# A hybrid decoder block on one core: the recurrence's gate products as three fp32r products of halves instead of one f32 product

## The chip, the cores and the metric

One of the eight cores of a Trainium2 chip runs one launch of the kernel. The metric is the device time of that launch in microseconds (us); lower is better. TensorE is called PE in the rows, its weight load PEld, VectorE DVE, ScalarE ACT, GpSimd POOL and SyncE SP.

## The reference, cut to what matters

One layer over 256 tokens of width 2048: a mixer (retention heads beside a gated linear recurrence, the RG-LRU), cross-attention into 256 memory tokens, a gated feed-forward part with a convolution, and norms between them. All is f32. The change is in the two gates of the RG-LRU:

```
def rg_lru(u, w_a, b_a, w_x, b_x, lam):
    ub = uf.reshape(B, S, LRU_BLOCKS, LRU_BLOCK_DIM)          # 8 blocks of 128
    r = sigmoid(einsum('bsnc,ncd->bsnd', ub, w_a) + b_a)
    i = sigmoid(einsum('bsnc,ncd->bsnd', ub, w_x) + b_x)
    log_a = LRU_C * r * log_sigmoid(lam)
    a = exp(log_a)
    b = sqrt(-expm1(2.0 * log_a)) * (i * uf)
    ... scan over the tokens: h = a * h + b
```

`u` is a causal convolution (4 taps) of a projection of the normed input. So each of 8 blocks needs two products of a 128x128 weight with a 128x256 input.

## The kernel before, in words

All weights of the large products come as one stream of panels, 128 partitions by 1024 f32, in the order of their use. SP loads a panel into one of four slots of `raw`; ACT copies it, rounded to fp32r, into `whi` (`split` at L560); DVE subtracts and writes the rest into `wlo` (`split` at L916). A product with f32 accuracy is then three fp32r products, high by high, high by low, low by high. A chunk is two panels; `narrow` (L273) is one chunk against all 256 tokens: 32 products, 16 of 512 columns (high half of the weight by both halves of the input) and 16 of 256 columns. `wide` (L290) does the same with weight and input exchanged.

Every engine has its own program, written out by hand, and semaphores between them. On ACT and DVE, `step(m, pr, do0, do1, do2)` waits until TensorE has used a pair of panels, calls `do0`, splits the first new panel, calls `do1`, splits the second, calls `do2`. An engine does its program strictly in the written order. The side work of a stage (copies, norms, taps) hangs in these three places.

The stage of the recurrence's projections is a loop over the 8 blocks, `n` from 0 to 7; one pass has two steps, for the chunk of `u` and the chunk of `y`:

- ACT, first step: `u0` asks for the block's gate weights (`gw`, a part of `dmask`, 128x256: both gates side by side) and copies half of the product's sum out of PSUM (`copy_hl`, L575); `u1` makes the first term of the convolution (L686). Second step: `copy_hl` again, then `y1` after `gates_done`: three tanh (L692 to L694); `y2` the gelu (L698).
- DVE, first step: `u0` adds the halves and scales (L934, L1096); `u1` adds the other three taps into `scr[:, 3]` (L1102) and signals `uc_ready`. Second step: `y0` (L934, L1111) and `y1` (L1117).
- TensorE: `gates_of(n)` (L382) stands inside the `narrow` of the next block, after its first 12 products, and for the last block after the first panel of the value projection that follows. It waits for `uc_ready` and for the weights, and makes two f32 products of 256 columns into `bankA`:

```
mm(bankA[:, :T], gw[:, :P], scr[:, 3, :], True, True)
mm(bankA[:, T:], gw[:, P:], scr[:, 3, :], True, True).then_inc(gates_done, 1)
```

The cross-attention, later, has products of the same form as the new ones: `scores` (L461) and `attend` (L481), fp32r halves with 256 columns.

Of the kernel before, what the change touches and what calls it, by code (L numbers as in the profile page):

```python
# [29 lines left out]
ALU = mybir.AluOpType  # L30
ACT = mybir.ActivationFunctionType
# [3 lines left out]
P = 128  # L35
D = 2048
T = 256
# [18 lines left out]
C_YU = C_KM + KT  # L56
# [60 lines left out]
def build(nc, stream, cols, xin, memin, xt_in, memt_in, first_in, pos, gates, decay, ident_in, gfin_in, out):  # L117
    with ExitStack() as ctx:
        def sb(name, shape, dt=F32):
            return ctx.enter_context(nc.sbuf_tensor(name, shape, dt))  # L120

        def sem(name):
            return ctx.enter_context(nc.semaphore(name))
# [24 lines left out]
        with ExitStack() as early:  # L148
            gel, dmask, scrg, scr, vbuf = (early.enter_context(nc.sbuf_tensor(n, shape, F32)) for n, shape in (
                ("gel", [P, LB, T]), ("dmask", [P, RH, T]), ("scrg", [P, 4, T]), ("scr", [P, 8, T]), ("vbuf", [P, TT, R])))  # L150
        k_head, q_hi, q_lo = sb("k_head", [P, 2, 4, T], F32R), sb("q_hi", [P, 4, T], F32R), sb("q_lo", [P, 4, T], F32R)
        sb("scr_low", [P, 2, T])
        p_head = sb("p_head", [P, 2, 2, T], F32R)
        sb("scr_high", [P, 2, T])
        v_heads = sb("v_heads", [P, 2, TT, XD], F32R)

        mem_rows = [b[:].rearrange("p a b -> p (a b)") for b in (vbuf, gel)]
        lru_t = xres[:, 0, :].rearrange("p (n t) -> p n t", n=LB)
# [3 lines left out]
        gw = dmask[:, 0, :]  # L162
# [7 lines left out]
        bankA, bankB = ps[:, 6, :], ps[:, 7, :]  # L170
# [16 lines left out]
        gw_in, un_ready, uc0_done, uc_ready, yn_ready, gates_done, i_ready = (  # L187
            sem(n) for n in ("gw_in", "un_ready", "uc0_done", "uc_ready", "yn_ready", "gates_done", "i_ready"))
# [9 lines left out]
        qT_ready, sc_done, nb_ready, p_ready, pn_ready, pt_done, pT_ready, v_ready, pv_done, ot_hi, ot_lo = (  # L198
            sem(n) for n in ("qT_ready", "sc_done", "nb_ready", "p_ready", "pn_ready", "pt_done", "pT_ready", "v_ready",
                             "pv_done", "ot_hi", "ot_lo"))  # L200
        q_sum, q_hi_done, k_hi_done, k_ready, p_hi_done, v_hi_done = (
            sem(n) for n in ("q_sum", "q_hi_done", "k_hi_done", "k_ready", "p_hi_done", "v_hi_done"))
        up_ready, cv_done, cva_ready, sil_done, hh_ready, hh_hi, hh_lo = (
# [4 lines left out]
        def f32(ap):  # L208
            return ap.bitcast(F32)
# [59 lines left out]
        def _(pe):  # L269
            def mm(o, l, r, start, stop):  # L270
                return nc.tensor.matmul(o, l, r, start=start, stop=stop, skip_group_check=True)  # L271
# [109 lines left out]

            def gates_of(n1):  # L382

                pe.wait_ge(uc_ready, n1)
                pe.wait_ge(gw_in, 16 * n1)
                mm(bankA[:, :T], gw[:, :P], scr[:, 3, :], True, True)
                mm(bankA[:, T:], gw[:, P:], scr[:, 3, :], True, True).then_inc(gates_done, 1)

            pe.wait_ge(xt_lo, KT - 2)
            narrow(C_YU // 2, 0, xT, {KT - 2: lambda: pe.wait_ge(xt_lo, KT)})  # L390
# [1 line left out]
            with pe.Fori(1, LB) as n:  # L392
                narrow(C_YU // 2 + n, 0, xT, {6: lambda: gates_of(n)})
                narrow(C_YU // 2 + n, 1, xT)

            for n, (g, kp) in enumerate(WIDE_ORDER):
                wide(C_V // 2 + n // 2, n % 2, xT, range(4 * kp, 4 * kp + 4), 2 * g, kp == 0, kp == 3,
                     None if n else lambda: gates_of(LB))
# [138 lines left out]
            for tt in range(TT):  # L537
                for n in range(2):
                    for k in range(GF):
                        if tt == 0 and k % 2 == 0:  # L540
                            pe.wait_ge(lo_done, 2 * NC - 4 + 2 * n + k // 2 + 1)
                        w = slice(k % 2 * CG, (k % 2 + 1) * CG)
# [4 lines left out]
                        last = mm(ps[:, 2 * n + tt, :], x_lo, hi, False, k == GF - 1)  # L547
# [4 lines left out]
        def _(act):  # L552
            ch = Chain(act, chain_a)
            A = nc.scalar.activation

            def split(m, pr, s):

                act.wait_ge(raw_landed[2 * pr + s], 16 * m + 32)
                act.wait_ge(panels_used, 4 * m + (2 * pr + s + 1))
                A(whi[:, 2 * pr + s, :], raw[:, 2 * pr + s, :], ACT.Copy).then_inc(hi_done, 1)  # L560

            def step(m, pr, do0=None, do1=None, do2=None):

                act.wait_ge(panels_used, 4 * m + (2 * pr + 2))
                if do0:
                    do0()
                split(m, pr, 0)
                if do1:
                    do1()
                split(m, pr, 1)  # L570
                if do2:
                    do2()

            def copy_hl(pr):
                A(hl[:, pr, :], ps[:, 4 + pr, T:], ACT.Copy).then_inc(hl_copied, 1)  # L575
# [101 lines left out]
            with act.Fori(0, LB) as n:  # L677
                ch.reg = n

                def u0():  # L680
                    act.dma_start(gw, gates[n]).then_inc(gw_in, 16)
                    copy_hl(0)

                def u1():
                    act.wait_ge(un_ready, n + 1)
                    A(scr[:, 3, :], scr[:, 2, :], ACT.Identity, scale=par[:, ds(4 * n + (O_CW + 3), 1)],  # L686
                      bias=par[:, ds(n + O_CB, 1)]).then_inc(uc0_done, 1)

                def y1():

                    act.wait_ge(gates_done, n + 1)
                    ch.link(A(scr[:, 4, :], bankA[:, :T], ACT.Tanh, scale=0.5, bias=halves[:, ds(n, 1)]))  # L692
                    A(scr[:, 5, :], bankA[:, T:], ACT.Tanh, scale=0.5, bias=halves[:, ds(n + LB, 1)]).then_inc(i_ready, 1)
                    ch.mark(A(lru_t[:, n, :], scr[:, 4, :], ACT.Tanh, scale=cs[:, ds(n, 1)], bias=cs[:, ds(n, 1)]))  # L694

                def y2():
                    act.wait_ge(yn_ready, n + 1)
                    A(gel[:, n, :], scr[:, 6, :], ACT.Gelu_apprx_tanh)  # L698

                step(C_YU // 2 + n, 0, u0, u1)  # L700
                step(C_YU // 2 + n, 1, lambda: copy_hl(1), y1, y2)
            ch.leave(LB)

# [206 lines left out]
        def _(dve):  # L910
            V = nc.vector
            ch = Chain(dve, chain_v)

            def split(m, pr, s):
                dve.wait_ge(hi_done, 4 * m + (2 * pr + s + 5))
                V.tensor_tensor(wlo[:, 2 * pr + s, :], raw[:, 2 * pr + s, :], f32(whi[:, 2 * pr + s, :]),  # L916
                                ALU.subtract).then_inc(lo_done, 1)

            def step(m, pr, do0=None, do1=None, do2=None):

                dve.wait_ge(panels_used, 4 * m + (2 * pr + 2))
                if do0:
                    do0()
                split(m, pr, 0)
                if do1:
                    do1()
                split(m, pr, 1)
                if do2:
                    do2()

            def narrow_sum(w, pr, dst):

                dve.wait_ge(hl_copied, w + 1)
                return V.tensor_tensor(dst, ps[:, 4 + pr, :T], hl[:, pr, :], ALU.add)  # L934
# [156 lines left out]
            with dve.Fori(0, LB) as n:  # L1091
                ch.reg = n

                def u0():
                    ch.link(narrow_sum(W_YU + 2 * n, 0, tmp[:, 0, :]))
                    V.tensor_tensor(scr[:, 2, :], tmp[:, 0, :], row[:], ALU.mult).then_inc(un_ready, 1)  # L1096

                def u1():
                    dve.wait_ge(uc0_done, n + 1)
                    for tap in (2, 1, 0):  # L1100
                        sh = 3 - tap
                        ins = V.scalar_tensor_tensor(out=scr[:, 3, sh:], in0=scr[:, 2, :T - sh],  # L1102
                                                     scalar=par[:, ds(4 * n + (O_CW + tap), 1)], in1=scr[:, 3, sh:],
                                                     op0=ALU.mult, op1=ALU.add)
                        if tap:
                            ch.link(ins)
                    ins.then_inc(uc_ready, 1)

                def y0():
                    ch.link(narrow_sum(W_YU + 2 * n + 1, 1, tmp[:, 1, :]))  # L1110
                    V.tensor_tensor(scr[:, 6, :], tmp[:, 1, :], row[:], ALU.mult).then_inc(yn_ready, 1)  # L1111

                def y1():
                    dve.wait_ge(i_ready, n + 1)
                    dve.wait_ge(uc_ready, n + 1)

                    V.scalar_tensor_tensor(out=lru_gx[:, n, :], in0=scr[:, 5, :], scalar=1.0, in1=scr[:, 3, :],  # L1117
                                           op0=ALU.add, op1=ALU.mult)

                step(C_YU // 2 + n, 0, u0, u1)  # L1120
                step(C_YU // 2 + n, 1, y0, y1)
            ch.leave(LB)

# [404 lines left out]
```

## Time and profile before

| what | value |
|---|---|
| median of 3 runs | 1505.83 us (1505.77 to 1506.15) |
| profiled execution | 1505.75 us |
| its span, first to last instruction | 1504.0 us |
| busy: PE, DVE, ACT | 1494.7, 1076.4, 818.5 us |
| granted TensorE clock, mean | 0.999 |
| the recurrence stage | about 188 to 284 us |

The profiled execution is taken by the hardware profiler; its own time is 1.75 us above its span. A clock of 1.00 is the full 2.4 GHz. In a timeline row stand start, length, engine, line, operation, output and inputs with shapes; a row with xN is N instructions in a row, its length from the first start to the last end. What stands in square brackets is the idle time before it and what ended it. Names like `scr` or `dmask` are the program's tensors, `ps` is PSUM. f32 and fp32r inputs of TensorE both read "f32".

### The profile page before, as it was taken

Reading aid. Unit: us, or ns where it says so; the run is one execution under the profiler, and the core shown is the slowest. Engines: PE = TensorE matmul, PEld = TensorE weight load, DVE = VectorE, ACT = ScalarE, POOL = GpSimd, SP = SyncE. Lnnn points to the kernel's source line nnn. Section 1 sums busy time; section 2 is a strip of 40 time slices with the busy share of each in tenths; the row PEclk is TensorE's granted clock in tenths of the full one; section 3 lists DMA queues with packets and bytes.
Section 4 is the critical chain, followed back from the end, with each engine's and each line's share of the span. In section 5 each row is a group of like instructions: output and inputs, shape, how many; then the busy total and the mean of one; then the engine's idle time right before and its main releaser. Section 6 shows DMA issues by size and latency. Waiting matters only on the chain.

```text
span 1504.0 us, 24205 instructions
## 1 busy us (share of the span) xinstructions
PE 1494.7 (99%) x7926; PEld 1282.6 (85%) x7926; DVE 1076.4 (72%) x1577; ACT 818.5 (54%) x1185; POOL 2.9 (0%) x9
## 2 busy tenths in 40 slices
PE   9999999999999999999999999999999999999997
PEld 8888888888888888888888888888888888888886
DVE  6756666788887556655578777777777777777876
ACT  6644478644555546544575455454645455454654
POOL 0000000000000000000000000000000000000000
PEclk9999999999999999999999999999999999999999
DMA  9766655655556554446556555555555555555553
GB/s 349 251 204 210 209 183 189 202 186 168 173 177 237 182 184 166 144 156 200 181 169 198 186 193 189 195 186 187 191 188 196 188 187 190 195 184 193 184 194 140
DMA packets 80458, 288.89 MB, mean 192 GB/s; under 512 B 8944, under 2 KB 10480, under 8 KB 79520
## 3 DMA queue, kind: packets, MB, share of 16 engines
q1 hardware_dynamic: 76176, 275.68, 55.3%
q10 hardware_dynamic: 3744, 9.30, 1.8%
q0 software_dynamic: 496, 3.34, 0.6%
q8 instruction: 27, 0.44, 0.1%
q14 instruction: 15, 0.12, 0.0%
HBM read 286.19 MB, written 2.10 MB: 192 GB/s over the span
## 4 chain that ended last, share of the span: by engine, by line
PE 97%; DVE 1%; ACT 1%; issue 0%; DMA 0%; ACTq 0%; DVEq 0%
PE ps L271 97%; PE ps L328 0%; DVE wlo L916 0%; ACT whi L560 0%; DVE vm L1399 0%; DMA hl<-in_first_in 0%; DVE xres L1409 0%; PE ps L423 0%; ACT scr L800 0%; ACT scr L893 0%; DVE sm_ L1268 0%; DVE xres L1372 0%; ACT vm L906 0%; PE ps L477 0%; DVE tmp L934 0%
## 5 line engine op out<-in xcount | busy, mean ns | idle before, releaser
L271 PE MATMUL ps<-xT,whi 128*128 128x512 f32 x2304 | 727.5, 397 | 0.2
L916 DVE TENSOR_TENSOR wlo<-raw,whi 128x1024 fp32r<-128x1024 f32 x516 | 623.0, 1221 | 127.5 <-ACT whi L560 117.9
L560 ACT ACTIVATE whi<-raw 128x1024 fp32r<-128x1024 f32 x516 | 531.8, 1050 | 224.3 <-PE ps L271 219.4
L271 PEld LDWEIGHTS ps<-xT,wlo 128*128 128x128 f32 x2304 | 432.8, 188 | 102.0
L271 PE MATMUL ps<-whi,mixT 128*128 128x512 f32 x1472 | 457.6, 390 | 0.2 <-ACT whi L601 0.2
L271 PE MATMUL ps<-xT,wlo 128*128 128x256 f32 x2304 | 453.0, 278 | 0.0
L271 PEld LDWEIGHTS ps<-xT,whi 128*128 128x128 f32 x2304 | 352.6, 189 | 2.3 <-DVE wlo L916 0.8
L271 PEld LDWEIGHTS ps<-whi,mixT 128*128 128x128 f32 x1472 | 276.3, 188 | 57.8 <-issue 0.6
L271 PE MATMUL ps<-wlo,mixT 128*128 128x512 f32 x736 | 285.2, 389 | 0.0
L575 ACT ACTIVATE hl<-ps 128x256 f32<-128x256 f32 x160 | 61.5, 384 | 236.6 <-PE ps L271 236.5
L934 DVE TENSOR_TENSOR tmp<-ps,hl 128x256 f32<-128x256 f32 x160 | 67.7, 423 | 146.3 <-ACT hl L575 146.0
L271 PEld LDWEIGHTS ps<-wlo,mixT 128*128 128x128 f32 x736 | 138.1, 188 | 27.8 <-DVE wlo L975 0.2
L1372 DVE TENSOR_TENSOR xres<-ps,xres 128x512 f32<-128x512 f32 x84 | 54.1, 686 | 60.5 <-PE ps L271 59.3
L1335 DVE SCALAR_TENSOR_TENSOR tmp<-tmp,par 128x255 f32<-128x255 f32 (+1 forms) x176 | 84.6, 481 | 11.1 <-DVE tmp L1335 1.5
L271 PE MATMUL ps<-mixT,whi 128*128 128x512 f32 x256 | 80.4, 395 | 0.0
L854 ACT ACTIVATE tmp<-tmp,par 128x256 f32<-128x256 f32 x88 | 53.0, 603 | 18.7 <-DVE tmp L1328 17.6
L271 PEld LDWEIGHTS ps<-mixT,wlo 128*128 128x128 f32 x256 | 48.1, 188 | 11.4
L863 ACT ACTIVATE mixT<-scr 128x256 fp32r<-128x256 f32 x44 | 18.4, 418 | 68.6 <-DVE scr L1345 39.1
L271 PE MATMUL ps<-mixT,wlo 128*128 128x256 f32 x256 | 50.3, 278 | 0.0
L271 PE MATMUL ps<-whi,xT 128*128 128x512 f32 x128 | 39.9, 391 | 0.0
L1328 DVE TENSOR_TENSOR tmp<-tmp,row 128x256 f32<-128x256 f32 x88 | 37.4, 425 | 3.0
L271 PEld LDWEIGHTS ps<-mixT,whi 128*128 128x128 f32 x256 | 39.0, 189 | 0.1
(177 smaller groups left out, 645.7 us busy)
## 6 DMA issues: line engine op xcount, KB each, us to landing
raw<-in_stream SPq DMA_DIRECT2D x518, 512.0 KB, 3.3
xres<-in_xin ACTq DMA_DIRECT2D x2, 1024.0 KB, 7.9
scr<-in_xt_in ACTq DMA_DIRECT2D x8, 256.0 KB, 3.6
xres<-in_xin POOLq DMA_DIRECT2D x1, 2048.0 KB, 9.9
out_x<-vm SPq DMA_DIRECT2D x4, 512.0 KB, 3.1
raw<-in_stream SPq DMA_DIRECT2D x4, 256.0 KB, 4.2
kT<-in_memt_in ACTq DMA_DIRECT2D x2, 512.0 KB, 5.3
vbuf<-in_memin ACTq DMA_DIRECT2D x1, 1024.0 KB, 9.7
```

What stands on the lines that cost most here:

```text
L271: return nc.tensor.matmul(o, l, r, start=start, stop=stop, skip_group_check=True)
L560: A(whi[:, 2 * pr + s, :], raw[:, 2 * pr + s, :], ACT.Copy).then_inc(hi_done, 1)
L575: A(hl[:, pr, :], ps[:, 4 + pr, T:], ACT.Copy).then_inc(hl_copied, 1)
L854: A(tmp[:, 2 + ab, :], tmp[:, ab, :], ACT.Identity, scale=par[:, ds(4 * u + (O_FC + 2), 1)], bias=par[:, ds(4 * u + (O_FC + 3), 1)]).then_ ...
L863: A(mixT[:, k0 + k, 0, :], hold[:, k % 2, :], ACT.Copy).then_inc(hh_hi, 1)
L916: V.tensor_tensor(wlo[:, 2 * pr + s, :], raw[:, 2 * pr + s, :], f32(whi[:, 2 * pr + s, :]), ALU.subtract).then_inc(lo_done, 1)
L934: return V.tensor_tensor(dst, ps[:, 4 + pr, :T], hl[:, pr, :], ALU.add)
L1328: V.tensor_tensor(tmp[:, ab, :], tmp[:, 5, :], row[:], ALU.mult).then_inc(up_ready, 1)
L1335: ins = V.scalar_tensor_tensor(out=tmp[:, 2 + ab, sh:], in0=tmp[:, ab, :T - sh], scalar=par[:, ds(4 * u + (O_FC + tap), 1)], in1=tmp[:, 2 ...
L1372: V.tensor_tensor(x, ps[:, 2 * (n % 2) + tt, :], x, ALU.add).then_inc(fin_added, 1)
```

## The change

The gate weights and the convolved input are each split in a high and a low half, into a buffer that lies idle in this stage (`q_lo`, whose place is that of `scrg`). ACT writes the high halves (two more copies a block), DVE the low halves (two more subtractions), both in the third place of the first step, and TensorE makes three fp32r products for each gate. It waits for one new semaphore, `gate_ready`, which DVE raises after the second subtraction. The weights' landing is now waited for by ACT.

```diff
+        gw_parts, u_parts = q_lo[:, 0:2, :], q_lo[:, 2:4, :]
...
+        gw_hi_done, u_hi_done, gate_ready = sem("gw_hi_done"), sem("u_hi_done"), sem("gate_ready")
...
             def gates_of(n1):
 
-                pe.wait_ge(uc_ready, n1)
-                pe.wait_ge(gw_in, 16 * n1)
-                mm(bankA[:, :T], gw[:, :P], scr[:, 3, :], True, True)
-                mm(bankA[:, T:], gw[:, P:], scr[:, 3, :], True, True).then_inc(gates_done, 1)
+                pe.wait_ge(gate_ready, n1)
+                for j in range(2):
+                    o, w = bankA[:, j * T:(j + 1) * T], slice(j * P, (j + 1) * P)
+                    mm(o, gw_parts[:, 0, w], u_parts[:, 0, :], True, False)
+                    mm(o, gw_parts[:, 0, w], u_parts[:, 1, :], False, False)
+                    last = mm(o, gw_parts[:, 1, w], u_parts[:, 0, :], False, True)
+                last.then_inc(gates_done, 1)
...
+                def u2():
+                    act.wait_ge(gw_in, 16 * n + 16)
+                    A(gw_parts[:, 0, :], gw, ACT.Copy).then_inc(gw_hi_done, 1)
+                    act.wait_ge(uc_ready, n + 1)
+                    A(u_parts[:, 0, :], scr[:, 3, :], ACT.Copy).then_inc(u_hi_done, 1)
...
-                step(C_YU // 2 + n, 0, u0, u1)
+                step(C_YU // 2 + n, 0, u0, u1, u2)
...
+                def u2():
+                    dve.wait_ge(gw_hi_done, n + 1)
+                    V.tensor_tensor(gw_parts[:, 1, :], gw, f32(gw_parts[:, 0, :]), ALU.subtract)
+                    dve.wait_ge(u_hi_done, n + 1)
+                    V.tensor_tensor(u_parts[:, 1, :], scr[:, 3, :], f32(u_parts[:, 0, :]), ALU.subtract).then_inc(gate_ready, 1)
...
-                step(C_YU // 2 + n, 0, u0, u1)
+                step(C_YU // 2 + n, 0, u0, u1, u2)
```

The order on DVE between the third tap (`scr<-scr,par 128x253`) and the scaling in `y0`, in the loop over the blocks, before and then changed (line numbers of the changed kernel are 2 to 17 higher):

```order
L1102 SCALAR_TENSOR_TENSOR scr<-scr,par 128x253
L915 REGISTER_ALU
L916 TENSOR_TENSOR wlo<-raw,whi 128x1024 [waits hi_done]
L921 REGISTER_ALU
L933 REGISTER_ALU [waits panels_used]
L934 TENSOR_TENSOR tmp<-ps,hl 128x256 [waits hl_copied]
L96 REGISTER_ALU
L1111 TENSOR_TENSOR scr<-tmp,row 128x256 [waits chain_v]
```

```order
L1113 SCALAR_TENSOR_TENSOR scr<-scr,par 128x253
L926 REGISTER_ALU
L927 TENSOR_TENSOR wlo<-raw,whi 128x1024 [waits hi_done]
L1122 TENSOR_TENSOR q_lo<-dmask,q_lo 128x256 [waits gw_hi_done]
L1124 TENSOR_TENSOR q_lo<-scr,q_lo 128x256 [waits u_hi_done]
L932 REGISTER_ALU
L944 REGISTER_ALU [waits panels_used]
L945 TENSOR_TENSOR tmp<-ps,hl 128x256 [waits hl_copied]
L96 REGISTER_ALU
L1128 TENSOR_TENSOR scr<-tmp,row 128x256 [waits chain_v]
```

Between the tap and the second subtraction, whose end TensorE now waits for, stand a panel's split and the first subtraction.

The order on ACT from the first term of the convolution to the tanh, changed kernel (`q_lo` is the buffer of the halves, `dmask` holds the gate weights):

```order
L691 ACTIVATE scr<-scr,par 128x256
L565 ACTIVATE whi<-raw 128x1024 [waits panels_used,raw_landed1]
L695 ISA
L696 ACTIVATE q_lo<-dmask 128x256 [waits gw_in]
L698 ACTIVATE q_lo<-scr 128x256 [waits uc_ready]
L569 REGISTER_ALU
L580 ACTIVATE hl<-ps 128x256 [waits panels_used]
L564 REGISTER_ALU [waits raw_landed2]
L565 ACTIVATE whi<-raw 128x1024 [waits panels_used]
L703 REGISTER_ALU [waits gates_done]
L703 ACTIVATE scr<-ps,halves 128x256
```

The two copies stand ahead of the hl copy and of the third split, which before followed the second split at once.

## Rows read from the trace of the kernel before

**Rows 1.** The first page: the span, and TensorE's busy time
```profile
span 1504.0 us, 24205 instructions
...
PE 1494.7 (99%) x7926; PEld 1282.6 (85%) x7926; DVE 1076.4 (72%) x1577; ACT 818.5 (54%) x1185; POOL 2.9 (0%) x9
```

**Rows 2.** Chain that ended last, 188 to 284 us: start, length, what
```profile
187.84 96.29 PE ps L271 x538
```

**Rows 3.** Busy time in two stretches: PE, PEld, DVE, ACT, POOL, then PE clock, DMA
```profile
0.00:10.00 10.00, 8.84 (x38) 7.80 (x39) 4.40 (x8) 6.10 (x11) 1.61 (x7) 1.00 0.79 282
188.00:284.00 96.00, 96.00 (x539) 83.57 (x538) 64.01 (x96) 74.49 (x102) 0.00 (x0) 1.00 0.56 184
```

**Rows 4.** Instructions on tile dmask: durations in ns, first and last start
```profile
L271 PE MATMUL ps<-scr,dmask x32: 377/378/379, 196.0 to 281.5; 128*128 128x256 f32 x32
...
DMA to landing us min/median/max: 2.2/3.5/5.5
```

**Rows 5.** Timeline of PE around one block's gates: start, length, engine, line, operation
```profile
255.44 0.63 PE L271 MATMUL ps<-xT,whi 128*128 128x512 f32 x2
255.91 0.40 PE L271 MATMUL ps<-xT,wlo 128*128 128x256 f32 x2
256.14 1.02 PE L271 MATMUL ps<-scr,dmask 128*128 128x256 f32 x4
...
257.47 0.40 PE L271 MATMUL ps<-xT,wlo 128*128 128x256 f32 x2
```

**Rows 6.** Timeline of PE around the attention's products of halves
```profile
599.94 3.02 PE L271 MATMUL ps<-p_head,v_heads 128*128 128x256 f32 x24
602.80 0.63 PE L271 MATMUL ps<-xT,whi 128*128 128x512 f32 x2
```

**Rows 7.** Timeline of PE, gate products of blocks 1, 5 and 8
```profile
196.04 1.02 PE L271 MATMUL ps<-scr,dmask 128*128 128x256 f32 x4
...
244.12 1.02 PE L271 MATMUL ps<-scr,dmask 128*128 128x256 f32 x4
...
280.82 1.02 PE L271 MATMUL ps<-scr,dmask 128*128 128x256 f32 x4
```

**Rows 8.** Timeline of ACT in one pass
```profile
245.28 0.47 ACT L692 ACTIVATE scr<-ps,halves 128x256 f32<-128x256 f32 x1 [1.72 <-PE ps L271]
...
248.81 0.34 ACTq L681 DMA_DIRECT2D dmask<-in_gates  x1
...
250.84 0.39 ACT L575 ACTIVATE hl<-ps 128x256 f32<-128x256 f32 x1
...
252.89 1.05 ACT L560 ACTIVATE whi<-raw 128x1024 fp32r<-128x1024 f32 x1
```

**Rows 9.** Timeline of DVE in the same pass
```profile
251.25 0.42 DVE L934 TENSOR_TENSOR tmp<-ps,hl 128x256 f32<-128x256 f32 x1 [2.19 <-ACT hl L575]
...
253.97 1.11 DVE L1102 SCALAR_TENSOR_TENSOR scr<-scr,par 128x254 f32<-128x254 f32 x2 [0.15 <-DVE scr L1102]
255.00 1.22 DVE L916 TENSOR_TENSOR wlo<-raw,whi 128x1024 fp32r<-128x1024 f32 x1
256.14 0.42 DVE L934 TENSOR_TENSOR tmp<-ps,hl 128x256 f32<-128x256 f32 x1
256.59 0.42 DVE L1111 TENSOR_TENSOR scr<-tmp,row 128x256 f32<-128x256 f32 x1
256.93 1.22 DVE L916 TENSOR_TENSOR wlo<-raw,whi 128x1024 fp32r<-128x1024 f32 x1
```

**Rows 10.** Timeline of DVE in the first pass: the split behind the taps
```profile
194.54 1.22 DVE L916 TENSOR_TENSOR wlo<-raw,whi 128x1024 fp32r<-128x1024 f32 x1
```

**Rows 11.** Timeline around a wait of TensorE for a DVE split
```profile
10.50 2.48 DVE L975 TENSOR_TENSOR wlo<-raw,whi 128x1024 fp32r<-128x1024 f32 x2 [1.00 <-ACT whi L605]
...
11.78 0.30 PEld L271 LDWEIGHTS ps<-wlo,mixT 128*128 128x128 f32 x2 [0.17 <-DVE wlo L975]
11.86 0.42 PE L271 MATMUL ps<-wlo,mixT 128*128 128x512 f32 x1
```

## The prediction

> **What bounds the kernel now.** I read the first page's busy shares and the chain of waits, then the stretch that the change touches. TensorE is busy for 1494.7 of 1504.0 us [rows 1], and in the stretch of the eight recurrence blocks (188 to 284 us) the chain that ended last is TensorE alone, with no wait in it [rows 2]. The table of that stretch says the same: PE 96.00 of 96.00 us, at the full granted clock of 1.00, with DVE at 64.01 and ACT at 74.49 [rows 3]. So one microsecond of TensorE saved here is one saved in the end, and any wait put into TensorE's stream here is lost in full, since nothing behind it stands idle to give it back. What has to be found is therefore two numbers: how much shorter the gate products get, and how late their inputs come.
>
> **Part 1, the products on TensorE.** Per block, two f32 products become six fp32r ones, all 256 columns wide. Before, the records show four entries of 377 to 379 ns for the two products (32 for the 16 of all eight blocks [rows 4]). In the sequence of TensorE a group opens with two products on the high half, the two on the low half start 0.47 us later (255.44 to 255.91), and the next group would open at 256.14. There the gate products stand, and that group's low half starts at 257.47 instead of 256.61: the two f32 products cost 257.47 - 256.14 - 0.47 = 0.86 us [rows 5]. The new shape has a row too: 24 products of 256 columns with fp32r halves in the attention fill 599.94 to 602.80, 2.86 / 24 = 0.119 us each [rows 6]. Six cost 0.715 us. Saving: 0.86 - 0.715 = 0.145 us a block, 8 x 0.145 = 1.2 us at most.
>
> The Trainium skill (FP8 and Floating Point Precision, TensorE Precision Notes) says that true FP32 takes 4 passes through the array, high and low halves against each other. The trace agrees as far as it goes: at 0.107 us for 256 columns at 2.4 GHz the pair's 0.86 us is eight passes. By that rule alone, three passes instead of four would save a quarter, 0.215 us a block or 1.7 us in all, and the sum below would be +4.6 us; I keep the 0.119 us of the row, which has the weight loads in it.
>
> **Part 2, where the inputs come from.** Before, the gate products waited for the third tap of the convolution alone (`uc_ready`). Now they wait for `gate_ready`, at the end of this: ACT copies the weights (128x256), waits for `uc_ready`, copies the convolved input; DVE takes first its next split of a weight panel (1.22 us), and only then the two subtractions. I follow the pass from 244.12 to 256.14.
>
> - Third tap: the last two taps run from 253.97 for 1.11 us, to 255.08. Room before TensorE asks, at 256.14: 1.06 us [rows 5, 9].
> - ACT's copies: its second split ends at 252.89 + 1.05 = 253.94 [rows 8]; the weights are asked for at 248.81 and land after 2.2 to 5.5 us [rows 4], by 254.3 at worst. A copy of 128x256 costs 0.39 us (the hl row [rows 8]): weights done by 254.7, the input's copy from 255.1 to 255.5. ACT's next work, another hl copy and a split, moves behind them: 255.5 + 0.39 + 1.05 = 256.9, before the gate products have begun. Off the path.
> - DVE: split from 255.00, next operation 1.14 us later at 256.14 [rows 9]. First subtraction 256.14, second 0.34 us later (the distance between an operation of 0.42 us and an independent next one, 256.59 to 256.93 [rows 9]), done at 256.48 + 0.42 = 256.90. ACT's copies are ready by then.
> - TensorE takes it up: at 11.78 a weight load starts some 0.04 us after the first of two DVE splits that released it (10.50 + 2.48 / 2 = 11.74), the product 0.08 us behind it [rows 11]. I take 0.15 us. First gate product at 257.05, against 256.14: late by 0.91 us.
>
> **Part 3, whether the wait repeats.** If only the inputs were late once, TensorE would slip by 0.9 us and be on time afterwards. But the next block's inputs hang on this block's gates. From the gates' end ACT has no pause: tanh at 245.28, three of them, a split, two loads of an activation table around the gelu, and the hl copy at 250.84 only when all this is done [rows 8]. DVE stood idle for 2.19 us for that very copy [rows 9]. Then follow the sum, the scaling, a split, the taps, the split and now the subtractions. So it is a closed loop: gates of block n, ACT's queue, DVE's queue, gates of block n+1. Before, its length was 255.08 - 244.12 = 10.96 us to `uc_ready`, and TensorE's own pass of 12.02 us (244.12 to 256.14 [rows 5, 7]) was the longer. Now it is:
>
>   257.05 - 244.12 = 12.93, less what the gates give back. Before, the tanh started 245.28 - 244.12 = 1.16 us after the first product. Six products at 0.119 put the last start at 0.60, its end 0.28 us later (3.02 - 23 x 0.119 [rows 6]) at 0.88, and the same 0.14 us to ACT makes 1.02. So 12.93 - 0.14 = **12.79 us**, against 11.87 that TensorE itself would need (12.02 - 0.145). The loop is the longer one, by 0.92 us a pass.
>
> **The sum.**
> - Block 1: third tap and split are at 194.54 [rows 10]; subtractions done at 194.54 + 1.14 + 0.34 + 0.42 = 196.44, first product at 196.59 instead of 196.04 [rows 7]: +0.55.
> - Blocks 2 to 7: six passes of 12.79 instead of 12.02: 6 x 0.77 = +4.62.
> - Block 8: its gates stand in the first panel of the value projection, 2.7 us into it instead of 2.1. 280.82 [rows 7] less 268.16 (196.04 + 6 x 12.02) is 12.66; the loop's 12.79 still wins: +0.13.
> - The last products: -0.145.
> Together 0.55 + 4.62 + 0.13 - 0.15 = **+5.15 us**. Counted the other way: waits 0.55 + 6 x 0.92 + 0.27 = 6.3 us, savings 1.2 us. After block 8 nothing else is changed, and TensorE carries the delay to the end.
>
> The profiled execution took 1505.75 us for its span of 1504.0; 1505.75 + 5.15 = 1510.9. The median of the runs is 1505.83, so the two stand together within 0.1 us. A measurement of this kernel can tell about 0.2%, 3.0 us, from no change; the forecast is above that.
>
> **Bounds of the unknown terms.** TensorE's start: 0.04 to 0.3 us. Distance of the two subtractions: 0.34, or 0.45 as between chained operations (256.14 to 256.59 [rows 9]). Tanh after the gates: the 0.14 us gain may be eaten by weight loads that cannot run ahead while TensorE waits. Low: 0.11 less on each of seven steps and 0.1 off the first, +4.3 us. High: 0.15 + 0.11 + 0.14 = 0.40 more on seven steps, 0.26 on the first, +8.2 us. I take the middle of the rows nearest to the new operations.
>
> **Rivals.**
> - *The room of 1.06 us covers it.* If the subtractions come before DVE's split, or nothing is late, only the saving is left: 1505.75 - 1.2 = 1504.6, no change that can be measured. For it: ACT and DVE are busy for only 78% and 67% of the stretch [rows 3]. Against: the order on DVE is fixed, and 1.14 + 0.34 + 0.42 after 255.00 is past 256.14 whatever the averages. It decides if `gate_ready` comes within 1.06 us of `uc_ready`; I count 1.82. Chance 0.08.
> - *The wait is paid once.* If the hl copy of the next block does not hang on the tanh, TensorE slips by 0.9 us once and saves 1.2: 1505.5. Against: ACT's rows from 245.28 to 250.84 have no gap. Chance 0.06.
> - *TensorE loses its clock.* Each pass would hold a stop of 0.9 us. The granted clock is 1.00 in the stretch and also in the first 10 us, where 1.16 us were idle [rows 3]. If a quarter of the stretch's 90 us ran at 1.2 instead of 2.4 GHz, it would take 22 us more: 1533. The Trainium skill (TensorE: Matmul & The Clock Gate, A second HAM failure mode: psum-queue depth-cycling) says that frequent short idles between groups of products can make the clock swing between its two levels. The row with 1.16 us idle in 10 speaks against it here. Chance 0.02.
> - *The loop is longer than I count*, at the high bound or beyond it: 1514. Chance 0.07, mostly inside the range.
>
> **How the numbers follow.** The forecast (a loop of about 12.8 us, seven times) has 0.77, and the predicted time is its 1510.9. The range takes its bounds, 1510.0 and 1514.0, with 0.6 us more below for a shorter wait on block 8 and on the first: 1509.4 to 1514.0. Left out are the first three rivals, 0.16, and little beyond the high bound. Slower by over 3.0 us: forecast, long loop and clock, 0.86. Within 0.2%: the first two rivals, 0.14, of which 0.01 goes to faster, for which I have no mechanism.
>
> **What would show it.** The view to read is TensorE from 188 to 290 us: eight waits before the gate products, released by DVE's second subtraction, about 0.55, 0.9 (six times) and 0.3 us, 6 us together; starts 12.8 us apart instead of 12.0; DVE's second subtraction ending 1.8 us behind the third tap; ACT without a gap from the tanh to the hl copy; the six products about 0.7 us; clock 1.00. No waits, or one only, would make me wrong, and so would starts 12.0 us apart.

## The result, and the profile after

The changed kernel takes 1511.11 us (median of 7 runs, 1510.81 to 1511.43), the kernel before beside it 1506.04 us (1505.75 to 1506.48): 5.1 us more, a ratio of 1.0034 with a 95% interval of 1.0025 to 1.0043. The forecast was 1510.9 us, in a range of 1509.4 to 1514.0. The profiled execution has a span of 1509.1 us where before had 1504.0 [rows 1].

The first page and the stretch of the recurrence, in the rows that answer to [rows 1] and [rows 3]; the stretch reaches to 290 us, since the stage is now longer:

```profile
span 1509.1 us, 24269 instructions
...
PE 1495.2 (99%) x7942; PEld 1282.4 (85%) x7942; DVE 1082.3 (72%) x1593; ACT 823.5 (55%) x1201; POOL 2.9 (0%) x9
```

```profile
188.00:290.00 102.00, 97.84 (x558) 84.35 (x557) 69.84 (x114) 80.19 (x119) 0.00 (x0) 1.00 0.51 175
```

TensorE's busy time has hardly moved (1494.7 us before), the span is 5.1 us longer, and 4.2 of the 102 us of the stretch are idle on TensorE, at a granted clock of 1.00 as before. The view of waits in that stretch names what it waits for (engine and line, released by, us in total, times, longest):

```profile
PEld ps L273 <- DVE q_lo L1124: 6.0, 8, 0.9
PE ps L273 <- DVE q_lo L1124: 4.2, 7, 0.7
```

L1124 is DVE's second subtraction. The weight-load row counts each wait from the end of the last load (6.0 us in eight waits), the product row from the modelled end of the last product, which lies later (4.2 us). The timeline of one pass of the changed kernel, TensorE's rows first (these answer to [rows 5, 7]):

```profile
234.93 0.98 PE L273 MATMUL ps<-q_lo 128*128 128x256 f32 x6 [0.64 <-DVE q_lo L1124]
247.71 0.98 PE L273 MATMUL ps<-q_lo 128*128 128x256 f32 x6 [0.64 <-DVE q_lo L1124]
247.71 0.77 PEld L273 LDWEIGHTS ps<-q_lo 128*128 128x128 f32 x6 [0.84 <-DVE q_lo L1124]
248.53 0.64 PE L273 MATMUL ps<-xT,whi 128*128 128x512 f32 x2
```

The first and the last group of gate products in the same trace:

```profile
196.61 0.97 PE L273 MATMUL ps<-q_lo 128*128 128x256 f32 x6 [0.29 <-DVE q_lo L1124]
...
286.05 0.98 PE L273 MATMUL ps<-q_lo 128*128 128x256 f32 x6
```

Then DVE and ACT around them (these answer to [rows 8, 9]):

```profile
244.74 1.11 DVE L1113 SCALAR_TENSOR_TENSOR scr<-scr,par 128x254 f32<-128x254 f32 x2 [0.15 <-DVE scr L1113]
245.77 1.22 DVE L927 TENSOR_TENSOR wlo<-raw,whi 128x1024 fp32r<-128x1024 f32 x1
245.88 0.42 ACT L698 ACTIVATE q_lo<-scr 128x256 fp32r<-128x256 f32 x1 [0.87 <-DVE scr L1113]
246.90 0.42 DVE L1122 TENSOR_TENSOR q_lo<-dmask,q_lo 128x256 fp32r<-128x256 f32 x1
247.24 0.42 DVE L1124 TENSOR_TENSOR q_lo<-scr,q_lo 128x256 fp32r<-128x256 f32 x1
248.82 0.47 ACT L703 ACTIVATE scr<-ps,halves 128x256 f32<-128x256 f32 x1 [1.30 <-PE ps L273]
```

```profile
250.30 1.05 ACT L565 ACTIVATE whi<-raw 128x1024 fp32r<-128x1024 f32 x1
251.37 1.28 ACT L709 ACT_TABLE_LOAD   x1
252.36 0.34 ACTq L686 DMA_DIRECT2D dmask<-in_gates  x1
252.66 0.42 ACT L709 ACTIVATE gel<-scr 128x256 f32 x1
253.08 1.28 ACT L580 ACT_TABLE_LOAD   x1
254.38 0.38 ACT L580 ACTIVATE hl<-ps 128x256 f32<-128x256 f32 x1
```

The passes are 247.71 - 234.93 = 12.78 us apart instead of 12.02. The third tap is done at 245.85, ACT's copy of the input at 246.30, and then that copy lies unused for 0.94 us, because DVE is in the split of a panel and then in the first subtraction. TensorE starts 0.05 us behind the end of the second one. On ACT there is no gap from the first tanh to the hl copy, 248.82 to 254.38; the rows of the other two tanh are left out above.

### The profile page after: what moved, and what is told of

The parts are those of the page before. It is cut to its first block, busy times and chain, and to the rows that moved or that the text cites. A ratio compares the mean times of both kernels' runs of the same rounds, so it can differ in the third digit from the quotient of the medians.

```text
span 1509.1 us, 24269 instructions
## 1 busy us (share of the span) xinstructions
PE 1495.2 (99%) x7942; PEld 1282.4 (85%) x7942; DVE 1082.3 (72%) x1593; ACT 823.5 (55%) x1201; POOL 2.9 (0%) x9
## 4 chain that ended last, share of the span: by engine, by line
PE 92%; ACT 3%; DVE 2%; issue 1%; ACTq 0%; DMA 0%; DVEq 0%
PE ps L273 91%; ACT whi L565 1%; DVE wlo L927 1%; ACT L580 1%; DVE scr L1113 0%; PE ps L330 0%; ACT L709 0%; ACT scr L691 0%; DVE vm L1416 0%; DMA hl<-in_first_in 0%; DVE q_lo L1122 0%; ACT scr L703 0%; ACT hl L580 0%; ACTq L686 0%; DVE xres L1426 0%
```

## The experiments

Ten kernels ran. One theory had to be told from three others. The closed loop: gates, ACT's queue, DVE's queue, next gates are one ring, and whatever is longer, ring or TensorE's own pass, sets the time of a pass. Against it: added work costs wherever it stands; the new products themselves are dear; the lateness is fixed in each block and has nothing to do with ACT's queue. The expectations count the kernels in the order in which they were built: the fourth is the one with the gelu out of the loop, the sixth and the seventh have the useless copy, in the changed kernel and in the kernel before.

### Subtractions ahead of the split

```diff
                     ins.then_inc(uc_ready, 1)
+                    dve.wait_ge(gw_hi_done, n + 1)
+                    V.tensor_tensor(gw_parts[:, 1, :], gw, f32(gw_parts[:, 0, :]), ALU.subtract)
+                    dve.wait_ge(u_hi_done, n + 1)
+                    V.tensor_tensor(u_parts[:, 1, :], scr[:, 3, :], f32(u_parts[:, 0, :]), ALU.subtract).then_inc(gate_ready, 1)
...
-                step(C_YU // 2 + n, 0, u0, u1, u2)
+                step(C_YU // 2 + n, 0, u0, u1)
```

> The changed kernel with DVE's two subtractions directly behind the third tap, ahead of the second split of a weight panel. Closed-loop theory: in the changed kernel the second subtraction starts 1.39 us behind the end of the third tap (245.85 to 247.24); here it starts as soon as ACT's copy of the input is done, about 0.50 us behind it, so the loop falls from 12.77 to about 11.9 us, a tie with TensorE's own pass of 11.87. The waits nearly vanish, the time is 1504.6 to 1505.6 us, 5.5 to 6.5 below the changed kernel and 0.2 to 1.2 below the kernel before. Rival, that the delay is the mere work added on ACT and DVE, wherever it stands: same work, so no change from the changed kernel, 1511. Rival, that the six products themselves are dearer than the row of the attention says: still above 1508.

Measured: 1504.93 us (11 runs, 1504.56 to 1505.54), before 1505.96; ratio 0.9993, interval 0.9984 to 1.0002. No wait of TensorE in the stretch. DVE and TensorE in this run:

```profile
253.68 1.11 DVE L1113 SCALAR_TENSOR_TENSOR scr<-scr,par 128x254 f32<-128x254 f32 x2 [0.15 <-DVE scr L1113]
254.70 0.42 DVE L1120 TENSOR_TENSOR q_lo<-dmask,q_lo 128x256 fp32r<-128x256 f32 x1
255.27 0.43 DVE L1122 TENSOR_TENSOR q_lo<-scr,q_lo 128x256 fp32r<-128x256 f32 x1 [0.15 <-ACT q_lo L698]
255.61 1.22 DVE L927 TENSOR_TENSOR wlo<-raw,whi 128x1024 fp32r<-128x1024 f32 x1
```

```profile
243.96 0.89 PE L273 MATMUL ps<-q_lo 128*128 128x256 f32 x6
255.84 0.89 PE L273 MATMUL ps<-q_lo 128*128 128x256 f32 x6
```

The first subtraction lies in the time in which DVE has to wait for ACT's copy anyway; the second ends at 255.70, the products start at 255.84 with no bracket behind them, and the pass is 11.88 us. All the work of the change is still done. So with ACT's queue as it is, it is not the work but its place in DVE's queue that costs 6.2 us (1511.11 - 1504.93).

### The wait kept, the f32 products back

```diff
                 pe.wait_ge(gate_ready, n1)
-                for j in range(2):
-                    o, w = bankA[:, j * T:(j + 1) * T], slice(j * P, (j + 1) * P)
-                    mm(o, gw_parts[:, 0, w], u_parts[:, 0, :], True, False)
-                    mm(o, gw_parts[:, 0, w], u_parts[:, 1, :], False, False)
-                    last = mm(o, gw_parts[:, 1, w], u_parts[:, 0, :], False, True)
-                last.then_inc(gates_done, 1)
+                mm(bankA[:, :T], gw[:, :P], scr[:, 3, :], True, True)
+                mm(bankA[:, T:], gw[:, P:], scr[:, 3, :], True, True).then_inc(gates_done, 1)
```

> The changed kernel, all copies, subtractions and the wait for gate_ready kept, but TensorE makes the two f32 products of before. Closed-loop theory: the products' part of the loop grows back by 0.1 to 0.14 us, so 12.9 us a pass, and the saving of 1.2 us is gone: 1512.0 to 1512.4 us, 0.9 to 1.3 above the changed kernel. If the new products were what costs the time, this would be near 1506.

Measured: 1512.17 us (5 runs, 1512.00 to 1512.63), ratio 1.0043, interval 1.0029 to 1.0056. Its passes:

```profile
235.25 1.13 PE L273 MATMUL ps<-scr,dmask 128*128 128x256 f32 x4 [0.66 <-DVE q_lo L1120]
248.18 1.13 PE L273 MATMUL ps<-scr,dmask 128*128 128x256 f32 x4 [0.66 <-DVE q_lo L1120]
```

12.93 us apart, 0.15 more than with the fp32r products. The wait alone is worth 6.2 us, and the products give 1.1 us of it back.

### The products alone

```diff
-                pe.wait_ge(gate_ready, n1)
+                pe.wait_ge(uc_ready, n1)
+                pe.wait_ge(gw_in, 16 * n1)
...
+            for j in range(8):
+                A(q_lo[:, j // 2, (j % 2) * P:(j % 2 + 1) * P], ones[:], ACT.Copy)
             act.wait_ge(halves_set, 1)
...
-                def u2():
```

(Shown against the changed kernel. `u2` is gone from both engines, so the halves are not made: the kernel leaves out the gates' values and its output is not that of the layer.)

> The kernel before with six fp32r products in place of the two f32 ones, waiting as before for uc_ready and the weights. The halves are left out: the products read a buffer filled once with ones, so the gates' values are left out of the computation. Closed-loop theory: no wait appears, the products cost 0.70 to 0.72 us instead of 0.86, TensorE's pass is 11.87 us, and the time is 1504.6 us, 1.2 below the kernel before (ratio 0.9992). If the products in this place cost what they do in the changed kernel's trace (0.82 us from the first product to the next group's), the gain is 0.3 us: 1505.5.

Measured: 1504.82 us (11 runs, 1504.59 to 1505.29), ratio 0.9992, interval 0.9983 to 1.0001. The products of a pass and the group behind them:

```profile
219.92 0.79 PEld L273 LDWEIGHTS ps<-q_lo 128*128 128x128 f32 x6
220.04 0.88 PE L273 MATMUL ps<-q_lo 128*128 128x256 f32 x6
220.75 0.63 PE L273 MATMUL ps<-xT,whi 128*128 128x512 f32 x2
221.04 0.48 ACT L700 ACTIVATE scr<-ps,halves 128x256 f32<-128x256 f32 x1 [1.57 <-PE ps L273]
```

0.71 us, and passes of 11.87 us (231.91 - 220.04 in the same view). This is all that the change can give: 1.1 us, and the first experiment gets nearly the same, 1.0 us, with the work of the splits in it. Both intervals still hold a ratio of 1, so the medians alone do not show a gain. The passes do: from the first to the eighth group of gate products it is 84.78 us in the kernel before (196.04 to 280.82), 83.75 us here and 83.81 us in the first experiment.

### The gelu out of the loop

```diff
-                def y2():
-                    act.wait_ge(yn_ready, n + 1)
-                    A(gel[:, n, :], scr[:, 6, :], ACT.Gelu_apprx_tanh)
...
+            def gelus(n0):
+                act.wait_ge(yn_ready, LB)
+                A(gel[:, n0:n0 + 4, :], gel[:, n0:n0 + 4, :], ACT.Gelu_apprx_tanh)
+
+            gelus(0)
...
-                    step(C_V // 2 + n // 2, 0, None, lambda: lru_root(n // 2))
+                    step(C_V // 2 + n // 2, 0, None, lambda: lru_root(n // 2), (lambda: gelus(4)) if n == 6 else None)
...
-                    V.tensor_tensor(scr[:, 6, :], tmp[:, 1, :], row[:], ALU.mult).then_inc(yn_ready, 1)
+                    V.tensor_tensor(gel[:, n, :], tmp[:, 1, :], row[:], ALU.mult).then_inc(yn_ready, 1)
```

> The changed kernel with the gelu taken out of the loop over the blocks (two instructions of four blocks each behind it), so that the gelu and the two table loads around it, 3.0 us, leave ACT's queue between the gates and the next hl copy. Nothing on the gates' inputs is changed. Closed-loop theory: the loop is 12.77 - 3.0 = 9.8 us, shorter than TensorE's pass, so all waits for gate_ready go and only the saving is left: 1504.6 us, at most 1.5 more if the gelus behind the loop delay a split. Rival, a fixed lateness of gate_ready that does not depend on ACT's queue (paid in each block since the inputs are 1.8 us behind the tap): the waits stay, 1511.

Measured: 1509.03 us (11 runs, 1508.66 to 1509.18), ratio 1.0020, interval 1.0011 to 1.0029. A miss by 4.4 us: only 2.1 us of the loss came back. The waits of TensorE are 0.28 us each in the timeline, and the passes 12.40. ACT shows why:

```profile
224.12 1.05 ACT L565 ACTIVATE whi<-raw 128x1024 fp32r<-128x1024 f32 x1
226.16 0.34 ACTq L686 DMA_DIRECT2D dmask<-in_gates  x1
226.54 1.28 ACT L580 ACT_TABLE_LOAD   x1 [1.36 <-PE ps L273]
227.83 0.39 ACT L580 ACTIVATE hl<-ps 128x256 f32<-128x256 f32 x1
```

One table load has stayed. It belongs to the hl copy at the head of the loop's body, and it cannot start before the copy's own wait, for TensorE's use of the panels. So the ring has changed its course: no longer by the tanh, but gates, the 20 products behind them, this load, hl copy, DVE. The hl copy stands 227.83 - 221.54 = 6.29 us behind the gates, against 254.38 - 247.71 = 6.67 us in the changed kernel: 0.38 us less, as the passes are. The sum in my expectation had taken both loads out.

### The same without the last table load

```diff
             act.wait_ge(halves_set, 1)
+            A(scr[:, 6, :8], ones[:, :8], ACT.Tanh)
             ch.enter(0, 2)
```

On top of the edit of the fourth run. The load then stands once, ahead of the loop (its row is in the last section).

> The changed kernel with the gelu out of the loop, as in the fourth run, plus one small tanh on ACT (128x8) ahead of the loop, so that no table load is left inside it. The fourth run kept one load a pass: it stood in front of the hl copy and began only when TensorE had used the panels (226.54 in that trace, hl copy at 227.83), and the passes were 12.40 us. Closed-loop theory, with this load as the rest of the loop: without it the hl copy comes 1.28 us sooner, gate_ready 12.40 - 1.28 = 11.12 us behind the gates before, under TensorE's 11.87; no wait is left and the time is 1504.8 to 1505.4 us. If the load is not what held the loop there, the passes stay at 12.4 us and the time at 1509.

Measured: 1504.85 us (11 runs, 1504.71 to 1505.02), before 1505.86; ratio 0.9993, interval 0.9983 to 1.0002. ACT now, and TensorE's passes of 11.87 us without a wait:

```profile
224.65 0.39 ACT L580 ACTIVATE hl<-ps 128x256 f32<-128x256 f32 x1 [1.40 <-PE ps L273]
224.94 1.05 ACT L565 ACTIVATE whi<-raw 128x1024 fp32r<-128x1024 f32 x1
```

```profile
219.72 0.88 PE L273 MATMUL ps<-q_lo 128*128 128x256 f32 x6
231.59 0.88 PE L273 MATMUL ps<-q_lo 128*128 128x256 f32 x6
```

```profile
227.79 1.11 DVE L1116 SCALAR_TENSOR_TENSOR scr<-scr,par 128x254 f32<-128x254 f32 x2 [0.15 <-DVE scr L1116]
228.82 1.22 DVE L930 TENSOR_TENSOR wlo<-raw,whi 128x1024 fp32r<-128x1024 f32 x1
229.95 0.42 DVE L1125 TENSOR_TENSOR q_lo<-dmask,q_lo 128x256 fp32r<-128x256 f32 x1
230.29 0.42 DVE L1127 TENSOR_TENSOR q_lo<-scr,q_lo 128x256 fp32r<-128x256 f32 x1
```

DVE's order is still that of the change, split first, and `gate_ready` still comes 1.81 us behind the tap (228.90 to 230.71), but now 0.88 us before TensorE asks. That the waits go all the same refutes a lateness fixed in each block.

### Control: the kernel before without the gelu in its loop

The same edit as in the fourth run, on the kernel before.

> Control: the kernel before with the same gelu taken out of the loop. Closed-loop theory: before, TensorE's pass of 12.02 us was the longer and had no wait, so a shorter loop gives nothing: 1505.8 us, ratio 1.000, unless the gelus behind the loop delay a split (up to 1.5 us more). If the gelu itself were a cost in both kernels, this would fall by several us as well.

Measured: 1506.48 us (11 runs, 1506.03 to 1506.83), before 1505.84; ratio 1.0003, interval 0.9994 to 1.0012. Not faster, the 0.6 us more within what was allowed for, and none of it in the loop: from the first to the eighth group of gate products it takes 84.78 us (196.35 to 281.13), exactly as before. The first group comes 0.31 us later than in the kernel before, by work ahead of the loop that the edit does not touch; the other 0.4 us of this execution lie behind the loop, and whether the moved gelus cause them was not tested. Shortening ACT's queue gives something only where the ring is the longer.

### A useless copy in the ring, in three kernels

```diff
                 def y2():
+                    A(tmp[:, 2:4, :], csr[:], ACT.Copy)
                     act.wait_ge(yn_ready, n + 1)
```

In the changed kernel:

> The changed kernel with one useless ACT copy of 128x512 (about 0.52 us) in each pass between the tanh and the gelu, a place that only the closed loop goes through. Closed-loop theory: each of seven passes gets longer by 0.52 us, +3.6 us: about 1514.7, and the waits of TensorE grow from 0.92 to 1.44 us. If the wait were paid once or came from elsewhere, the copy would cost nothing: 1511.1.

Measured: 1514.68 us (5 runs, 1514.52 to 1515.20), ratio 1.0058, interval 1.0045 to 1.0072: 3.6 us above the changed kernel. Two passes:

```profile
236.76 0.97 PE L273 MATMUL ps<-q_lo 128*128 128x256 f32 x6 [1.10 <-DVE q_lo L1125]
250.04 0.97 PE L273 MATMUL ps<-q_lo 128*128 128x256 f32 x6 [1.10 <-DVE q_lo L1125]
```

13.28 us, 0.51 more than without the copy.

In the kernel before:

> The same useless ACT copy in the kernel before. Closed-loop theory: the loop has 1.06 us of room there, and the first split of the next chunk 0.6 us, so the copy costs nothing: 1505.8 to 1506.2 us. If ACT's work in this place costs time by itself (memory traffic, say), it is 3.6 us here too: 1509.5.

Measured: 1506.71 us (11 runs, 1506.12 to 1507.05), before 1505.84; ratio 1.0004, interval 0.9995 to 1.0013. Passes of 12.06 us (256.76 - 244.69 = 12.07 in its timeline), so the copy costs 0.04 us of its about 0.5 a pass; some 0.4 us of the 0.9 is a later start of the whole loop (first gates at 196.44 instead of 196.04). It came out 0.5 us above what was expected, not the 3.6 of the other theory. No view shows a wait for the 0.04 us, so their cause stays open.

In the kernel with the subtractions ahead of the split:

> The first run's kernel (subtractions ahead of the split) with the useless ACT copy of 128x512 of the sixth and seventh runs. In the first run's trace the second subtraction ends at 255.69 and the gate products start at 255.84, about 0.1 us of room. Closed-loop theory: the copy's 0.52 us come out in nearly every pass, 7 x 0.43 = 3.0 us: about 1508, passes of 12.3 us. If the room there were as in the kernel before (1 us), nothing: 1505.

Measured: 1508.04 us (11 runs, 1507.87 to 1508.53), before 1505.86; ratio 1.0014, interval 1.0005 to 1.0023. 3.1 us above the first experiment:

```profile
233.26 0.98 PE L273 MATMUL ps<-q_lo 128*128 128x256 f32 x6 [0.21 <-DVE q_lo L1123]
245.64 0.98 PE L273 MATMUL ps<-q_lo 128*128 128x256 f32 x6 [0.21 <-DVE q_lo L1123]
```

The same copy costs 3.6, 0.9 and 3.1 us in the medians. Counted from the first to the eighth group of gate products alone it is 3.5, 0.3 and 3.1 us:

| kernel | without the copy | with it |
|---|---|---|
| changed | 89.44 us | 92.98 us |
| before | 84.78 us | 85.09 us |
| subtractions ahead of the split | 83.81 us | 86.90 us |

That goes with the room that each ring has: none, about one microsecond, about 0.1.

### Both mends at once

The first and the fourth edit together.

> The changed kernel with both mends, subtractions ahead of the split and the gelu out of the loop. Closed-loop theory: one mend is enough, so the same as the better of the two, 1504.6 us, no wait for gate_ready in the trace. If each hid only part of a wait, this would be below both by more than 0.5 us.

Measured: 1505.27 us (11 runs, 1504.97 to 1505.88), ratio 0.9996, interval 0.9987 to 1.0005; passes of 11.87 us, no wait. No better than the first edit alone, as expected. The time is 0.7 us above the expected 1504.6 and 0.3 us above the first experiment, but not in the loop: its eight groups span 83.75 us, there 83.81.

## Why the prediction was right

- **The wait repeats.** This step carries the forecast, and it held: a wait before each of the eight groups (the last, of 0.42 us, stands in the weight-load row alone), passes of 12.77 to 12.79 us for a predicted 12.79, the first block +0.45 instead of +0.55 (196.61, with the loop itself starting 0.12 later in this execution), the eighth product group at 286.05, 5.23 us behind before's 280.82, for a predicted 5.30. The copies and the last table load taken out show that the ring is real: it lengthens by 0.51 us a pass for about 0.5 us of copy, and with ACT's part cut the waits are gone.
- **The order on DVE.** Predicted 1.82 us from the tap to the end of the second subtraction, measured 247.66 - 245.85 = 1.81. The rival with the room of 1.06 us failed exactly there, and the first experiment is that rival made true: the subtractions ahead of the split, and only the saving left.
- **The products.** Predicted 0.715 us in place of 0.86. Without a wait they take 0.71 (third experiment); behind a wait 0.82 (247.71 to 248.53). In the stream the first weight load starts 0.12 us ahead of the first product (219.92 and 220.04, third experiment); behind the wait both start at 247.71, so the load falls into the time of the products.
- **Two sizes were off and cancel.** TensorE's take-up was set at 0.15 us and is 0.05. The tanh was set 1.02 us behind the first product and stands 1.11 behind (247.71 to 248.82). Each alone would have moved the time by 0.6 to 0.7 us. The two errors are most likely one and the same 0.1 us, of the first weight load: the prediction put it in front of the product's start, as in [rows 11], and behind a wait the trace records the product's start at the load's start. In the stream of the third experiment the tanh does start 1.00 us behind the product (220.04 to 221.04). What the ring needs is the sum, from the end of the subtraction to the tanh: 0.15 + 1.02 = 1.17 us predicted, 248.82 - 247.66 = 1.16 measured. That the take-up was rounded up to 0.15, from the 0.12 of [rows 11], and that this fits to 0.01 us, is luck.
- **The pass rule.** The price of four passes against three would have made the products 0.645 us; the 0.71 of the third experiment says that the row of the attention was the better price. The Trainium skill (FP8 and Floating Point Precision, TensorE Precision Notes) counts four passes for true FP32; the trace agrees for the f32 pair, whose 0.86 us is eight times 0.107, but the six products cost more than 6 x 0.107 = 0.64 us.
- **The clock** stayed at 1.00 with a stop in every pass. The Trainium skill (TensorE: Matmul & The Clock Gate, A second HAM failure mode: psum-queue depth-cycling) warns of swings of the clock from short idles; waits of 1.10 us in the product rows in every 13.28 us (the useless copy in the changed kernel) brought none here, the granted clock in its stretch from 188 to 295 us is 1.00.
- **What was wrong** was an expectation behind it, in the fourth run: the 3.0 us of gelu and table loads do not leave the loop together, one load of 1.28 us stays.

## What to carry to other kernels

Where an engine that is never idle waits for inputs that others make, ask whether those inputs hang, round the other engines' queues, on what that engine has just done. If they do, compare the ring's length with the engine's own pass: while the ring is the shorter, added work in it is nearly free (0.04 us of 0.5 a pass here), and where it is the longer, every microsecond is paid in every pass (0.51 of 0.5), and a mean busy share of 67% or 78% says nothing about it. Put short work that the bound engine waits for ahead of long work that it does not yet need: here the order of two subtractions and a split is worth 6.2 us.

## What the runs showed of the hardware that was not expected

With the gelu out of the loop a table load on ACT still stood in front of the first operation of the loop's body and was executed in every pass: 1.28 us each time (226.54 in the fourth run), though no operation that was left in the loop needed a change of table. One small tanh ahead of the loop removed it. That the load is there because the table on entering the loop was another one than the body's is a reading of these two runs; no other loop was tried. The load then stands once, before the loop:

```profile
186.03 1.28 ACT L681 ACT_TABLE_LOAD   x1
```

With it went 4.2 us (1509.03 to 1504.85; 4.1 us of span in the traces): six passes shorter by 0.53 us, the last by 0.10, the first block without its 0.45 us, and about 0.3 us by which this execution reached the loop sooner, which is not the edit's.

And six fp32r products cost 0.71 us in a stream and 0.82 behind a wait, by the 0.11 us of the first weight load.
